# Six filler tiles moved from behind to ahead of and between the first RWKV products of the second layer

## What is computed

```
for l in range(DEPTH):
    h = rms_norm(x, norm_g[l]);  p = h @ w_in[l]
    z, p_rw, p_ml, p_mla, p_da = _split(p, IN_WIDTHS)
    ...
    y = concat(beta_A*A, beta_B*B, beta_C*C, beta_D*D) * silu(z)
    x = x + y @ w_out[l]
```

```
p = _token_shift(p, mu);  r, k, v, wd, ad = _split(p, ...)
decay = jnp.exp(-jnp.exp(-jax.nn.softplus(-(w0 + jnp.tanh(wd) @ w_up)) - 0.5))
a = jax.nn.sigmoid(a0 + ad @ a_up)
v = v + (v_first - v) * jax.nn.sigmoid(v0 + (v @ v_dn) @ v_up)   # second layer only
kk = k * k_k, normalised per head;  k = k * (1.0 + (a - 1.0) * k_a)
```

## Time and profile before

| | us |
|---|---|
| median of 3 runs (lowest, highest) | 2259.07 (2257.66, 2260.38) |
| the profiled execution | 2262.43 |
| its span, first to last instruction | 2260.6 |
| PE busy | 2222.9 |
| POOL busy | 1744.9 |
| DVE busy | 1098.5 |

### The profile page before, as it was taken

The page is one execution under the profiler, slowest core; times in us unless marked ns, Lnnn a source line. Parts: engine busy times, 40 slices in busy tenths (PEclk is TensorE's granted clock), DMA queues, the critical chain, the costliest instruction groups (busy, mean ns, idle before and its releaser), DMA issues. The chain is left out here.

```text
span 2260.6 us, 35476 instructions
## 1 busy us (share of the span) xinstructions
PE 2222.9 (98%) x14528; PEld 1710.5 (76%) x14528; DVE 1098.5 (49%) x1475; ACT 668.8 (30%) x1217; POOL 1744.9 (77%) x1228
## 2 busy tenths in 40 slices
PE   7999999999999999999999999999999999999999
PEld 5767777777778778777777677767777787777777
DVE  5023327576574762555260223276666647525542
ACT  5222322222221332442342232223233213324421
POOL 3677679688688999888537776886797799898884
PEclk9999999999999999999999999999999999999999
DMA  5723344333234545622436233433333354466223
GB/s 164 193 74 94 94 136 123 95 115 104 92 108 155 162 140 189 242 91 82 147 104 177 84 103 89 142 111 100 99 115 97 90 176 150 131 209 225 92 83 127
DMA packets 165475, 288.44 MB, mean 128 GB/s; under 512 B 28792, under 2 KB 36344, under 8 KB 163776
## 3 DMA queue, kind: packets, MB, share of 16 engines
q1 hardware_dynamic: 125216, 211.60, 31.2%
q10 hardware_dynamic: 40096, 74.57, 9.9%
HBM read 234.43 MB, written 51.68 MB: 127 GB/s over the span
## 5 line engine op out<-in xcount | busy, mean ns | idle before, releaser
L753 POOL TENSOR_SCALAR w_hi<-raw 128x512 fp32r<-128x512 f32 x552 | 907.9, 1645 | 315.6 <-PE ps_proj L794 269.4
L763 POOL TENSOR_TENSOR w_lo<-raw,w_hi 128x512 fp32r<-128x512 f32 (+1 forms) x640 | 842.8, 1317 | 152.9 <-ACT w_hi L1230 97.5
L794 PE MATMUL ps_proj<-h_hi,w_hi 128*128 128x512 f32 (+1 forms) x1760 | 724.6, 412 | 6.9 <-POOL w_lo L763 4.2
L794 PE MATMUL ps_proj<-h_lo,w_hi 128*128 128x512 f32 (+1 forms) x1760 | 688.3, 391 | 0.0
L794 PE MATMUL ps_proj<-h_hi,w_lo 128*128 128x512 f32 x1728 | 675.6, 391 | 0.0
L794 PEld LDWEIGHTS ps_proj<-h_hi,w_hi 128*128 128x128 f32 (+1 forms) x1760 | 329.7, 187 | 105.3 <-issue 26.7
L794 PEld LDWEIGHTS ps_proj<-h_lo,w_hi 128*128 128x128 f32 (+1 forms) x1760 | 329.3, 187 | 73.1
L794 PEld LDWEIGHTS ps_proj<-h_hi,w_lo 128*128 128x128 f32 x1728 | 325.8, 189 | 66.3 <-issue 7.7
L809 PE MATMUL ps_proj<-w_hi,h_hi 128*128 128x512 f32 x448 | 181.3, 405 | 0.4 <-POOL w_lo L763 0.4
L809 PE MATMUL ps_proj<-w_lo,h_hi 128*128 128x512 f32 x448 | 174.8, 390 | 0.0
L809 PE MATMUL ps_proj<-w_hi,h_lo 128*128 128x512 f32 x448 | 174.8, 390 | 0.0
(11 more groups left out here) (344 smaller groups left out, 2884.0 us busy)
## 6 DMA issues: line engine op xcount, KB each, us to landing
raw<-in_w_in_dram SPq DMA_DIRECT2D x480, 256.0 KB, 2.7
raw<-in_w_out_dram SPq DMA_DIRECT2D x128, 256.0 KB, 3.0
projected<-stage SPq DMA_DIRECT2D x116, 256.0 KB, 2.8
arena<-projected ACTq DMA_DIRECT2D x90, 256.0 KB, 3.0
out_dram<-arena ACTq DMA_DIRECT2D x7, 1024.0 KB, 4.7
gated_hi<-arena ACTq DMA_DIRECT2D x24, 256.0 KB, 2.6
gated_lo<-arena ACTq DMA_DIRECT2D x24, 256.0 KB, 3.1
h_hi<-gated_hi SPq DMA_DIRECT2D x8, 768.0 KB, 5.9
```

The lines of the kernel that those rows point to most:

```text
L753: nc.gpsimd.tensor_scalar(hi, src, 1.0, None, ALU.mult).then_inc(s_hi_split, 1)
L763: nc.gpsimd.tensor_tensor(lo, src, hi.bitcast(F32), ALU.subtract).then_inc(s_raw_split, 1)
L794: last = mm(ps_proj[rows, m, :], lhsT, rhs, start=(k == 0 and j == 0), stop=(k == KT - 1 and j == len(products) - 1))
```

## The change

In the second layer `rw_first` gets 18 tiles in place of 14, a new place `rw_vdn` between line 971's products and the wait for their copy gets 2, and `rw_factors` of the first head pair gets 20 in place of 26. `rw_lora` keeps its 7. The first layer has 0 at the new place. ACT runs through the same plan for tiles that end a group; none of these do.

```diff
-    rw_first=8, rw_lora=(13, 11, 11, 11), rw_factors=(26, 28, 28, 28), rw_turned=(5, 5, 5, 5),
+    rw_first=8, rw_vdn=0, rw_lora=(13, 11, 11, 11), rw_factors=(26, 28, 28, 28), rw_turned=(5, 5, 5, 5),
...
-LATER_LAYERS = dict(FILL, rw_first=14, rw_lora=(7, *FILL["rw_lora"][1:]))
+LATER_LAYERS = dict(FILL, rw_first=18, rw_vdn=2, rw_lora=(7, *FILL["rw_lora"][1:]),
+                    rw_factors=(FILL["rw_factors"][0] - 6, *FILL["rw_factors"][1:]))
...
     place("rw_first")
+    place("rw_vdn")
...
                         last.then_inc(s_rw_vdn_mm, 1)
+                        fill("rw_vdn")
                         pe.wait_ge(s_rw_vd_ready, 1)
```

More of the change, by code:

```diff
@@ L1447, in _ @@
                     fill("rw_first")
+                    if mixes_v:
+                        fill("rw_vdn")
                     for hp in range(4):
```

## The result

The changed kernel took 2265.88 us (median of 10 runs, 2263.05 to 2266.61) against 2259.64 (10 runs, 2256.32 to 2262.18) for the kernel before: ratio 1.0022, 95% interval 1.0014 to 1.0031. Timed again later against the kernel before it took 2265.08 and that one 2260.41, ratio 1.0021 (1.0012 to 1.0030). So it is slower by 0.2%, some 4.9 us (0.00215, the mean of the two, x 2260; the medians of the two timings lie 6.2 and 4.7 us apart). The forecast was 2261.2, no change that can be told, in a range up to 2263.8; the measured time lies 2.1 us above that range.

A forecast was written before the change was run, and what follows sets the result against it. PE, busy 98%, was taken as the bound, with DVE's chain setting the transposes: +0.4 us (chain) + 1.65 (clock at the transposes) = +2.1, so median 2261.2, no change that can be told; range over the cases 2256.8 to 2263.8.

The forecast's parts named there:

- Products of 3.60 us at full clock: Values' products on PE: with 0.90 us of idleness before them the clock holds, 3.60 us in place of 5.29.
- POOL without a stop: POOL's splits: buffers given back earlier, so its stop from 1488.47 to 1493.65 goes and none is left before 1515.
- the chain longer beside POOL: DVE's chain of factors: 1.58 to 2.39 us longer with POOL busy beside it, taken as 26.7 us against 24.55.
- the fillers out at 1510.17: PE behind the sum of squares: out of fillers after 20 tiles, at about 1510.1.
- the new wait for the chain's last instruction: PE before the transposes: idle some 5.5 us, from 1510.1 to 1515.8, until DVE's chain ends.
- The transposes moved: PE's first transpose: starts at 1515.8, 0.4 us later than now (from 0.1 earlier to 0.7 later).
- The wait that takes the place of the old ones: PE's new idle before the transposes: clock falls to 1.2 GHz there, costing 1.65 us (bounds 0 to 3.3).
- All of it gained: Rival: old waits and low clock at the values' products go, 5.2 us gained, to 2253.9; chance 3%.
- DVE not slowed: Rival: DVE's chain stays near 24.55 us, transposes 1.7 us earlier, 2257.4 or 2259.0 by the clock there; chance 17%.
- The low clock at the products as well: Rival: products still take 5.29 us, chain 2.1 longer, low clock at transposes 1.65; +3.8, 2262.9; chance 11%.

The follow-up runs named there:

- after_again: The changed kernel, nothing further changed, profiled once more; this execution took 2264.29 us.
- after4: The changed kernel, nothing further changed, in a further profile; this execution took 2263.76 us.
- again2: The kernel before, unchanged, in a further profile; this execution took 2260.83 us.
- again3: The kernel before, unchanged, in a further profile; this execution took 2259.15 us.
- again5: The kernel before, unchanged, in a further profile; this execution took 2260.23 us.

## Why the prediction was wrong

**What held.** Products of 3.60 us at full clock (3.60 to 3.62 in all four profiles); POOL without a stop until 1515.6; the chain longer beside POOL (25.65 to 26.14 against 24.55, and 23.38 with POOL held); the fillers out at 1510.17 (1510.1); the new wait for the chain's last instruction, 4.34 to 4.39 us (forecast 5.5); the fall of the clock behind it. The transposes moved by +0.2 us on average over the profiles (forecast +0.4), but this agreement is in part luck. Against the mean of before the copy ended 0.9 us earlier, not 1.7, and the chain was 1.1 us longer, not 2.2; the two errors cancel.

**What failed: the term of the clock in "The wait that takes the place of the old ones".** It was priced at 1.65 us, half of one low stretch of 3.3 us of work. Measured it is 2.2 on average over the four profiles (7.59 less 5.36; 1.6 in after_again, 2.6 in after4): the low level had begun inside the wait and lasted 5.0 to 5.4 us into the work in three of the four. That lies in the bounds given (0 to 3.3), but the sum used the middle. This accounts for 0.6 of the 2.8 us between the forecast's +2.1 and the timed +4.9; with +0.2 at the transposes for +0.4 the stretch is +2.4, near the sum. The larger part of the miss lies in the base and in what stays open.

**And the base of the sum.** It was made on one execution, in which the shift was 3.47 us late and the products ran at the low clock. In three of the six profiles of before the shift is 2.25 us late, in one of them (again2) the clock holds, and the Gram products come 1.3 to 2 us earlier. The idle that the four tiles were to fill was 2.4 us in half of the executions, not 3.6, and there the tiles hold the products back (in after_again the products wait for PE's tiles, not for the shift). Against the mean of before the stretch costs 2.4 us; from the profiled execution of before to that of the change it grew by only 1.6 (41.24 less 39.69), less than the forecast 2.1. These two executions still lie 3.4 us apart (2265.87 against 2262.43): behind the stretch they differ by 2.0 us more, and there the clock fell at the end of the second layer in that of the change alone. The sum left the falls at the layers' ends at nothing, as equal before and after.

**What stays open.** The stretch gives 2.4 us of the 4.9 timed, and 1.3 more are in the profiles outside of it, nearly all in how often the clock fell at the layers' ends, half of that ahead of the change. The last 1.2 are the profiled executions of before, slower than its timed ones. The timed intervals (from 1.0012, 2.7 us, up) don't quite reach down to the stretch alone. Useless work in the wait and POOL held each took back all of it, so that wait is needed for the loss; but whether the falls at the second layer's end come oftener because of the change, three of four profiles against two of six don't settle.

**The rivals.** All of it gained: no, the transposes stayed. DVE not slowed: no. The low clock at the products as well: its time (2262.9) came nearest, but the products kept the full clock. What this rival gave as its way past 0.2%, a low level over more than 4.8 us of PE's work at the transposes, did occur in three of the four profiles. With the transposes 0.2 us later it makes 2.4 us in the stretch, about half of the bound of 4.5; that the time passed the bound, given 7%, needed the part left open as well.

## What to carry to other kernels

Where fillers and another engine's chain both end at one point, tiles taken from behind the chain's start shorten nothing: count what the other engine still needs, and move its work (here the shifts into its own wait, or the neighbour that contends) before moving fillers. A wait of 3.1 or 4.4 us before the transposes also cost the clock behind it, where those of 0.2 to 2.5 us there did not; 18 useless matmuls in it were worth as much as the whole loss. And before a sum is made against one profile, take two or three: the lateness of DVE's shift decided here whether PE waited 2.4 or 3.6 us at the products, and a fall of the clock far from the change was worth 1.7 us.

## What was not expected of the hardware

A wait of 2.4 us let the clock fall in two of three executions with the same instructions around it (again3 and again5, not again2), and one of 2.20 us at a layer's end in some executions of every set; the fall can come inside the wait or after work has begun (0.1 us behind the first transpose in after_again). DVE's six instructions took 4.24 us with POOL still and 6.5 to 7.0 beside it in the four profiles of the change, a factor of about 1.6. The end of DVE's shift against PE's fourteenth tile fell near three values (0.64, 2.25, 3.5 us) over seventeen profiles, with no value between; why is not known.
